# One 128x128 matrix in place of two parts of it, and a start in halves: a change to a two-layer decoder trunk

## The chip, the cores and the metric

The kernel is one program on one core of a Trainium2 chip. TensorE (PE in the rows) multiplies into PSUM, VectorE (DVE) and ScalarE (ACT) work on SBUF and PSUM, GpSimd (POOL) here only fills memory, and SyncE (SP) issues nearly all DMAs. Each engine runs its own instructions in order and waits for the others at semaphores. The metric is device time in microseconds.

## What is computed

Two layers over 256 tokens of width 1024, in float32. Each layer is a mixer with three branches (a short convolution, attention, and a delta rule with decaying state), a norm, a feed-forward part (dense in the first layer, two of eight experts in the second) and a norm. The change is about the delta rule and about the start of the first projection:

```python
def hybrid_mixer(x, w_in, ...):
    proj = x @ w_in
    (c_h, c_b, c_c, q, k, v, rr, rk, rv, wl, al, gl,
     g_conv, g_att, g_rwkv) = split_cols(proj, IN_SPLITS)
    ...

def delta_rule_scan(r, w, k, v, kk, a):
    def step(S, inp):
        r_t, w_t, k_t, v_t, kk_t, a_t = inp
        sa = jnp.einsum('bhvk,bhk->bhv', S, -kk_t)
        S = S * w_t[:, :, None, :] + sa[..., None] * (kk_t * a_t)[:, :, None, :] + v_t[..., None] * k_t[:, :, None, :]
        return S, jnp.einsum('bhvk,bhk->bhv', S, r_t)
    ...
    _, y = lax.scan(step, S0, xs)
```

## The kernel before

**Projections.** `x @ w_in` is worked off in units of 256 output columns. A unit's weight tile of 128 x 2048 (eight row blocks of 128 by 256 columns) is loaded by SyncE in two DMAs of 512 KB into one of three `raw` buffers. ScalarE copies it to `w_hi` (rounded), VectorE writes the rest, `raw - w_hi`, to `w_lo`, and TensorE makes each product as three (`mm3`, lines 471 to 473: hi by lo, lo by hi, hi by hi). A unit is two column blocks `m` of 128, each summed over eight row blocks `k` in one half of a PSUM bank `W[j % 3]`: 48 products. ScalarE then takes the bank out (`out_of_bank`, line 1163). The semaphores are `hi_done` and `lo_done` (tiles split so far), `w_used` (units multiplied so far) and `bank_free`. A tile is loaded two to three units ahead: the load of unit `u` waits until unit `u - 3` has been split (lines 323, 324). VectorE and ScalarE split unit `u + 2` while TensorE works on unit `u`.

**The order.** `TIMELINE` is a list written by hand. Each engine goes through it and does its own part of every entry. Small steps of the mixers stand between the units, or between a unit's first column block (`front`) and its second (`back`).

**The start.** SyncE issues, in this order: x part 0, first half of tile 0 (row blocks 0 to 3), x part 1, second half of tile 0, x parts 2 and 3, tile 1, the parameters, tile 2, a small weight, tile 3, the constants. ScalarE and VectorE split x in four parts and tile 0 in two halves. Tile 1 is split whole. TensorE's unit 0 runs the first column block over all `k`, waiting for the second half of the tile at `k = 4`, and then the second column block. After units 0, 1 and 2 comes `lora_w` (line 587), a product that needs `lora_in`: two ScalarE functions (lines 1203, 1204) on the result of unit 0, shifted by VectorE (`shift(6)`, lines 1676 to 1680). On VectorE that shift stands behind the split of tile 3.

**The delta rule.** It is done in two passes a layer, `p`, of four heads each, over two chunks `c` of 128 tokens. Every head and chunk (eight in a pass) has a triangular 128x128 matrix whose inverse is wanted. It is built in seven levels (`level`): two diagonal blocks of 64x64, and in the last level (`TOP`, lines 703 and 714) the block that joins them. They are kept transposed in `xt`, shape [128, 8, 2, 64], where the third index is the column half: `xt[0:64, :, 0]` and `xt[64:128, :, 1]` hold the diagonal blocks, `xt[0:64, :, 1]` the joining one. The lower diagonal block is made in `xt[64:128, :, 0]` and ScalarE copies it over (line 1318, `column_ready`). So `xt[64:128, :, 0]`, which would be zero in the transposed inverse, holds a used copy. VectorE writes the joining block (line 1792). Then, for each chunk, `cg` makes the right side and ScalarE copies it to `g_s`; `cu` applies the inverse to it; ScalarE copies that to `u_s`; `cy` makes output and state. `cu` therefore takes two products for each head: rows 0 to 63 of the result from partitions 0 to 63 of `xt` alone (line 738), rows 64 to 127 from all 128 partitions (line 739). There are eight `cu` groups in the kernel: two layers, two passes, two chunks.

In `TIMELINE`, `level(p, 6)`, `front` of a unit, `cg`, `back` of it and `cu` follow one another, and the same for the second chunk. GpSimd's program is five memsets at the start.

Of the kernel before, what the change touches and what calls it, by code (L numbers as in the profile page):

```python
# [32 lines left out]
P = 128  # L33
# [133 lines left out]
def trunk(nc, x, x_t, w_in, w_branch, w_out, w2, gate_w2, par, const, const_att, const_moe, ln_gb,  # L167
          router, ffn_gate, ffn_up, ffn_down, moe_gate, moe_up, moe_down, out):
    ctx = ExitStack()
    with ctx:  # L170
# [145 lines left out]
        def _(sp):  # L316
# [47 lines left out]
            def load_first_half(k, full):  # L364
                d = raw[0][:].rearrange("p (k c) -> p k c", k=KD)
                s = w_in[0][:, SEGMENTS[0][1]:SEGMENTS[0][1] + 256].rearrange("(k p) c -> p k c", p=P)
                sp.dma_start(d[:, k:k + 4, :], s[:, k:k + 4, :]).then_inc(sem(full), 16)

            load_x(0)
            load_first_half(0, "first_full0")  # L370
            load_x(1)
            load_first_half(4, "first_full1")
            load_x(2)
            load_x(3)
            for l in range(L):
                for kind, where, n, _ in SEGMENTS:
# [11 lines left out]
                    else:  # L388
                        for q in range(n):
                            if u + q:  # L390
                                load_cols(u + q, 0, w_in[l], where + 256 * (RKV[q] if kind == "rkv" else q))
# [76 lines left out]
        def _(pe):  # L468
# [22 lines left out]
            def proj_unit(u, j, fresh=None, parts=(0, 1)):  # L491

                if 0 in parts:
                    if u:
                        unit_ready(u)
                    else:
                        pe.wait_ge(sem("first_lo"), 1)
                    job_bank(j)
                bank = tiles(W[j % 3][:])
                wh, wl = (w[u % 3][:].rearrange("p (k c) -> p k c", k=KD) for w in (w_hi, w_lo))  # L500
                for m in parts:
                    c = slice(m * P, (m + 1) * P)
                    for k in range(KD):
                        if u == 0 and m == 0 and k == KD // 2:
                            unit_ready(0)
# [225 lines left out]
            def cu(l, p, c):  # L731
# [409 lines left out]
        def _(act):  # L1141
# [3 lines left out]
            def split_hi(u, i=0):  # L1145

                act.wait_ge(raw_full[u % 3], UD * (u // 3 + (1 if u % 3 else 0) + i))
# [10 lines left out]
            def out_of_bank(kind, q, u, j):  # L1158
# [3 lines left out]
                       "qkv": share[:, 2 * q:2 * q + 2, :]}.get(kind, sgate[:, (2 * q) % KD:(2 * q) % KD + 2, :])  # L1162
                A(dst, tiles(W[j % 3][:]), ACT.Sigmoid if kind.startswith("gate") else ACT.Copy)\
# [369 lines left out]
            act.wait_ge(sem("eps_ready"), 1)  # L1533
            def x_high(k):
# [3 lines left out]

            x_high(0)
            act.wait_ge(sem("first_full0"), 16)  # L1540
            A(w_hi[0][:, 0:UN // 2], raw[0][:, 0:UN // 2], ACT.Copy).then_inc(sem("first_hi"), 1)
            x_high(1)
            act.wait_ge(sem("first_full1"), 16)
            A(w_hi[0][:, UN // 2:UN], raw[0][:, UN // 2:UN], ACT.Copy).then_inc(hi_done, 1)
            x_high(2)
            x_high(3)
            split_hi(1)
# [54 lines left out]
        def _(pool):  # L1602
# [5 lines left out]
            nc.gpsimd.memset(s_s[:], 0.0).then_inc(sem("state_zero"), 1)  # L1608

# [3 lines left out]
        def _(dve):  # L1613
# [527 lines left out]
            def x_low(k):  # L2141
# [4 lines left out]

            x_low(0)
            dve.wait_ge(sem("first_hi"), 1)
            V.tensor_tensor(w_lo[0][:, 0:UN // 2], raw[0][:, 0:UN // 2], w_hi[0][:, 0:UN // 2].bitcast(F32), ALU.subtract)\  # L2149
                .then_inc(sem("first_lo"), 1)  # L2150
            x_low(1)
            dve.wait_ge(hi_done, 1)
            V.tensor_tensor(w_lo[0][:, UN // 2:UN], raw[0][:, UN // 2:UN], w_hi[0][:, UN // 2:UN].bitcast(F32), ALU.subtract)\
                .then_inc(lo_done, 1)
            x_low(2)
            x_low(3)
            split_lo(1)
# [102 lines left out]
```

## Time and profile before

| | us |
|---|---|
| median of 3 runs | 1743.91 |
| lowest and highest | 1743.23, 1744.04 |
| the profiled execution | 1743.99 |
| its span | 1741.9 |
| mean granted TensorE clock | 0.983 |

The span goes from the first to the last instruction; the profiled execution's own time is 2.1 us longer. TensorE is busy for 96% of the span, VectorE for 73%, ScalarE for 57%. In the timeline a product in fp32 that is not split stands as two passes of the same line, so `x8` of line 728 is four products. A busy time is that of the pipelined instruction from start to end; the pace of products is read from one start to the next. The three `mm3` lines of a unit start 0.12 us apart at the full clock.

### The profile page before, as it was taken

To read this page: it belongs to the slowest core of one execution; us is meant where nothing else is said; L and a number is where in the kernel's file an instruction comes from. 1 tells how busy PE (TensorE), PEld (TensorE's weight loads), DVE (VectorE), ACT (ScalarE), POOL (GpSimd) and SP (SyncE) were. 2 spreads that over 40 slices of the span, in tenths; PEclk is the share of its full clock that TensorE was granted. 3 is DMA by queue.
4 is the path that set the end of the run, shared out by engine and by line. 5 is a ranking of instruction groups with operands and counts; after the bars stand their busy time and mean duration, and the time that the engine had idled before them with its cause. 6 is when DMAs were issued, how large, how long until landed. Compare 5 with 4: busy or idle time off the path is not lost.

```text
span 1741.9 us, 30534 instructions
## 1 busy us (share of the span) xinstructions
PE 1680.4 (96%) x12126; PEld 1493.4 (86%) x12126; DVE 1274.5 (73%) x1217; ACT 1001.4 (57%) x967; POOL 0.9 (0%) x8
## 2 busy tenths in 40 slices
PE   7999999999999899999998999999999999999997
PEld 7899888889999889988987888888888888888886
DVE  5766666474444676656647889888998989888987
ACT  5553453453434555345344777777777777777775
POOL 0000000000000000000000000000000000000000
PEclk9999999999999899999998999999999999999999
DMA  9433332456656353333245999999998999899993
GB/s 285 146 98 119 100 121 75 163 170 193 187 174 213 126 163 105 98 121 122 75 145 207 340 333 392 333 371 368 346 386 325 374 331 392 333 367 350 368 385 142
DMA packets 253187, 411.19 MB, mean 236 GB/s; under 512 B 9376, under 2 KB 134688, under 8 KB 252576
## 3 DMA queue, kind: packets, MB, share of 16 engines
q1 hardware_dynamic: 250832, 400.97, 65.5%
q10 hardware_dynamic: 2256, 8.82, 1.4%
q8 instruction: 72, 1.18, 0.3%
q14 instruction: 27, 0.22, 0.0%
HBM read 407.66 MB, written 2.10 MB: 235 GB/s over the span
## 4 chain that ended last, share of the span: by engine, by line
PE 85%; DVE 7%; ACT 4%; issue 2%; DMA 1%; SPq 0%; ACTq 0%; DVEq 0%
PE W L471 18%; PE W L473 18%; PE W L472 18%; PE Y L471 6%; PE Y L472 6%; PE Y L473 6%; PE Y L675 3%; ACT w_hi L1150 2%; PE W L580 1%; DMA raw<-w_in 1%; DVE w_lo L1625 1%; DVE sc L1767 1%; PE Y L662 1%; PE Y L946 1%; PE Y L580 1%
## 5 line engine op out<-in xcount | busy, mean ns | idle before, releaser
L1625 DVE TENSOR_TENSOR w_lo<-raw,w_hi 128x2048 fp32r<-128x2048 f32 x114 | 261.2, 2292 | 218.2 <-ACT w_hi L1150 217.4
L471 PE MATMUL W<-w_lo,x_hi 128*128 128x512 f32 (+1 forms) x1120 | 390.3, 349 | 1.4 <-DVE x_lo L1928 1.1
L473 PE MATMUL W<-w_hi,x_hi 128*128 128x512 f32 (+1 forms) x1120 | 386.2, 345 | 0.0
L472 PE MATMUL W<-w_hi,x_lo 128*128 128x512 f32 (+1 forms) x1120 | 385.7, 344 | 0.0
L1632 DVE TENSOR_TENSOR w_lo<-raw,w_hi 128x2048 fp32r<-128x2048 f32 x144 | 329.6, 2289 | 44.9 <-ACT w_hi L1156 44.8
L1156 ACT ACTIVATE w_hi<-raw 128x2048 fp32r<-128x2048 f32 x144 | 276.0, 1917 | 73.3 <-PE Y L473 40.0
L471 PE MATMUL W<-x_lo,w_hi 128*128 128x256 f32 x992 | 296.8, 299 | 10.1 <-DVE w_lo L2149 8.9
L1632 DVE TENSOR_TENSOR w_lo<-raw_more,w_hi 128x2048 fp32r<-128x2048 f32 x120 | 274.9, 2291 | 28.7 <-ACT w_hi L1156 28.1
L472 PE MATMUL W<-x_hi,w_lo 128*128 128x256 f32 x992 | 286.4, 289 | 0.0
L473 PE MATMUL W<-x_hi,w_hi 128*128 128x256 f32 x992 | 285.9, 288 | 0.0
L1156 ACT ACTIVATE w_hi<-raw_more 128x2048 fp32r<-128x2048 f32 x120 | 230.5, 1921 | 64.0 <-PE W L473 41.3
L1150 ACT ACTIVATE w_hi<-raw 128x2048 fp32r<-128x2048 f32 x114 | 217.5, 1908 | 41.4 <-PE Y L473 31.2
L471 PEld LDWEIGHTS W<-w_lo,x_hi 128*128 128x128 f32 x1120 | 213.0, 190 | 26.8 <-issue 1.3
L473 PEld LDWEIGHTS W<-w_hi,x_hi 128*128 128x128 f32 x1120 | 212.8, 190 | 25.6
L472 PEld LDWEIGHTS W<-w_hi,x_lo 128*128 128x128 f32 x1120 | 213.0, 190 | 24.7
L471 PEld LDWEIGHTS W<-x_lo,w_hi 128*128 128x128 f32 x992 | 195.8, 197 | 19.1 <-DVE w_lo L2149 8.9
L472 PEld LDWEIGHTS W<-x_hi,w_lo 128*128 128x128 f32 x992 | 196.0, 198 | 1.3 <-issue 1.0
L473 PEld LDWEIGHTS W<-x_hi,w_hi 128*128 128x128 f32 x992 | 195.9, 198 | 0.0
L471 PE MATMUL Y<-w_lo,o_hi 128*128 128x512 f32 x440 | 172.3, 392 | 0.7 <-DVE o_lo L1942 0.7
L472 PE MATMUL Y<-w_hi,o_lo 128*128 128x512 f32 x440 | 171.5, 390 | 0.0
L473 PE MATMUL Y<-w_hi,o_hi 128*128 128x512 f32 x440 | 171.3, 389 | 0.0
L471 PEld LDWEIGHTS Y<-w_lo,o_hi 128*128 128x128 f32 x440 | 82.7, 188 | 17.4 <-DVE w_lo L1625 1.1
(318 smaller groups left out, 1929.7 us busy)
## 6 DMA issues: line engine op xcount, KB each, us to landing
raw<-w_in SPq DMA_DIRECT2D x124, 512.0 KB, 4.6
raw<-moe_gate SPq DMA_DIRECT2D x48, 1024.0 KB, 5.9
raw<-moe_up SPq DMA_DIRECT2D x48, 1024.0 KB, 6.3
raw<-moe_down SPq DMA_DIRECT2D x48, 1024.0 KB, 5.1
raw_more<-moe_gate SPq DMA_DIRECT2D x40, 1024.0 KB, 7.2
raw_more<-moe_up SPq DMA_DIRECT2D x40, 1024.0 KB, 6.7
raw_more<-moe_down SPq DMA_DIRECT2D x40, 1024.0 KB, 5.7
raw<-w_branch SPq DMA_DIRECT2D x24, 512.0 KB, 4.4
```

Source lines behind the costliest of these rows:

```text
L471: nc.tensor.matmul(out_ap, lhs[0], rhs[1], start=start, stop=False)
L472: nc.tensor.matmul(out_ap, lhs[1], rhs[0], start=False, stop=False)
L473: return nc.tensor.matmul(out_ap, lhs[0], rhs[0], start=False, stop=stop)
L580: return nc.tensor.transpose(out_ap, in_ap, ident)
L662: last = nc.tensor.matmul(Y[(1 + u + h) % 4][:, part], keys[rows, m, tc], ar[rows, m, c].rearrange("p s t -> p (s t)"), start=True, stop=True)
L675: last = nc.tensor.matmul(tiles(bank, 4)[half, u, :], left[half, 4 * c + u, :], right[half, 4 * c + u, :], start=True, stop=True)
L946: nc.tensor.matmul(out_ap, xs_lo[:, t, kk], picked, start=t == 0, stop=False)
L1150: A(w_hi[u % 3][:], raw[u % 3][:], ACT.Copy).then_inc(hi_done, 1)
L1156: A(w_hi[(u + x) % 3][:], landing(place_of(x))[:], ACT.Copy).then_inc(hi_done, 1)
L1625: V.tensor_tensor(w_lo[u % 3][:], raw[u % 3][:], w_hi[u % 3][:].bitcast(F32), ALU.subtract)\
L1632: V.tensor_tensor(w_lo[r][:], landing(place_of(x))[:], w_hi[r][:].bitcast(F32), ALU.subtract).then_inc(lo_done, 1)
L1767: mark(V.tensor_tensor(sc[:, u].rearrange("p (b s) t -> p b (s t)", b=2), tiles(Y[(1 + u) % 4][:]), si, ALU.mult), "score_ready", 8 * n + ...
```

## The change

1. `cu`: one product for each head with the whole of `xt[:, 4c+h]` as a 128x128 matrix, in place of two with parts of it. For this `xt[64:128, :, 0]` must be zero: GpSimd clears it with a memset in each of the four passes, after the column was copied and the last level's products have read it, and `cu` waits for that (`corner_clear`) and no longer for the copy.
2. Unit 0 on TensorE: both column blocks over row blocks 0 to 3, then both over 4 to 7. The second block's sum lies in `Y[0]`, so that ScalarE takes the unit out with two copies.
3. Tile 1 is split in halves like tile 0, each with a semaphore of its own, and unit 1 begins when the first half is split.
4. ScalarE makes a copy of one column of `small` ahead of everything.

```diff
-            def load_first_half(k, full):
-                d = raw[0][:].rearrange("p (k c) -> p k c", k=KD)
+            def load_first(u, k):
+                d = raw[u][:].rearrange("p (k c) -> p k c", k=KD)
+                col = SEGMENTS[u][1]
...
             load_x(0)
-            load_first_half(0, "first_full0")
+            load_first(0, 0)
             load_x(1)
-            load_first_half(4, "first_full1")
+            load_first(0, 4)
             load_x(2)
             load_x(3)
+            load_first(1, 0)
+            load_first(1, 4)
...
+                if u == 0:
+                    for half in range(2):
+                        if half:
+                            unit_ready(0)
+                        else:
+                            pe.wait_ge(sem("first_lo"), 1)
+                        for m, to in enumerate((bank[:, 0, :], tiles(Y[0][:])[:, 0, :])):
+                            c = slice(m * P, (m + 1) * P)
+                            for k in range(4 * half, 4 * half + 4):
+                                if m == 0:
+                                    x_part(0, k)
+                                last = mm3(to, (wh[:, k, c], wl[:, k, c]), (x_hi[:, k, :], x_lo[:, k, :]),
+                                           k == 0, k == KD - 1)
+                    last.then_inc(w_used, 1)
+                    return
+                if u == 1:
+                    pe.wait_ge(sem("first_lo"), 2)
+                elif 0 in parts:
+                    unit_ready(u)
...
                 if c == 0:
-                    pe.wait_ge(sem("column_ready"), n + 1)
+                    pe.wait_ge(sem("corner_clear"), n + 1)
                 for h, m, hc, half in HEADS:
-                    nc.tensor.matmul(Y[1][0:HD, hc], xt[0:HD, 4 * c + h, 0, :], g_s[0:HD, h, :], start=True, stop=True)
-                    last = nc.tensor.matmul(Y[1][HD:P, hc], xt[:, 4 * c + h, 1, :], g_s[:, h, :], start=True, stop=True)
+                    whole = xt[:, 4 * c + h].rearrange("p a b -> p (a b)")
+                    last = nc.tensor.matmul(Y[1][:, hc], whole, g_s[:, h, :], start=True, stop=True)
...
+                if u == 0:
+                    A(dst[:, 0, :], W[0][:, 0:T], ACT.Copy)
+                    A(dst[:, 1, :], Y[0][:, 0:T], ACT.Copy).then_inc(bank_free[0], 1)
+                    return
...
             act.wait_ge(sem("eps_ready"), 1)
+            A(small[:, 52:53], small[:, 9:10], ACT.Copy)
...
             x_high(3)
-            split_hi(1)
+            first_hi(1, 0)
+            first_hi(1, 4)
...
+            pool.wait_ge(sem("state_zero"), 1)
+            for n in range(2 * L):
+                if n:
+                    pool.wait_ge(sem("corner_clear"), n)
+                pool.wait_ge(sem("column_ready"), n + 1)
+                pool.wait_ge(sem("dxt_done"), 2 * TOP * (n + 1))
+                nc.gpsimd.memset(xt[HD:P, :, 0, :], 0.0).then_inc(sem("corner_clear"), 1)
```

TensorE at the first `cu` group, before: the last product of the unit's second block, then the products of the group (eight of them, two for each head; the first three stand here).

```order
L472 MATMUL W<-x_hi,w_lo_56 128x256
L473 MATMUL W<-x_hi,w_hi_53 128x256
L738 MATMUL Y<-gu_s,xt 64x64
L739 MATMUL Y<-gu_s,xt 64x64
L738 MATMUL Y<-gu_s,xt 64x64
```

The same place now, up to the next unit.

```order
L475 MATMUL W<-x_hi,w_lo_56 128x256
L476 MATMUL W<-x_hi,w_hi_53 128x256
L757 MATMUL Y<-gu_s,xt 128x64 x4
L474 MATMUL W<-x_lo,w_hi_54 128x256
L475 MATMUL W<-x_hi,w_lo_57 128x256
```

Nothing has moved here: eight products of at most 64 result rows have become four of 128.

ScalarE at the start, before; the names in brackets are the semaphores waited for.

```order
L1537 ACT_TABLE_LOAD [waits x_full0]
L1537 ACTIVATE x_hi<-xf 128x512 [waits eps_ready]
L1541 ACTIVATE w_hi_52<-raw_49 128x1024 [waits first_full0]
L1537 ACTIVATE x_hi<-xf 128x512 [waits x_full1]
L1544 ACTIVATE w_hi_52<-raw_49 128x1024 [waits first_full1]
L1537 ACTIVATE x_hi<-xf 128x512 [waits x_full2]
L1537 ACTIVATE x_hi<-xf 128x512 [waits x_full3]
L1150 ACTIVATE w_hi_53<-raw_50 128x2048 [waits raw_full1]
L1150 ACTIVATE w_hi_54<-raw_51 128x2048 [waits raw_full2]
```

ScalarE at the start now.

```order
L1556 ACT_TABLE_LOAD
L1556 ACTIVATE small<-small 128x1 [waits eps_ready]
L1560 ACTIVATE x_hi<-xf 128x512 [waits x_full0]
L1565 ACTIVATE w_hi_52<-raw_49 128x1024 [waits first_full00]
L1560 ACTIVATE x_hi<-xf 128x512 [waits x_full1]
L1565 ACTIVATE w_hi_52<-raw_49 128x1024 [waits first_full04]
L1560 ACTIVATE x_hi<-xf 128x512 [waits x_full2]
L1560 ACTIVATE x_hi<-xf 128x512 [waits x_full3]
L1565 ACTIVATE w_hi_53<-raw_50 128x1024 [waits first_full10]
L1565 ACTIVATE w_hi_53<-raw_50 128x1024 [waits first_full14]
L1168 ACTIVATE w_hi_54<-raw_51 128x2048 [waits raw_full2]
```

The table load no longer waits for x, and tile 1 is copied in two halves. VectorE's splits follow in the same order.

## Rows read from the trace of the kernel before

**Rows 1.** The page: busy time by engine, and the chain's shares by engine

```profile
PE 1680.4 (96%) x12126; PEld 1493.4 (86%) x12126; DVE 1274.5 (73%) x1217; ACT 1001.4 (57%) x967; POOL 0.9 (0%) x8
...
PE 85%; DVE 7%; ACT 4%; issue 2%; DMA 1%; SPq 0%; ACTq 0%; DVEq 0%
```

**Rows 2.** The chain of waits at the groups: start us, us, what

```profile
185.43 0.45 PE Y L580 x4
...
193.38 0.70 DVE rkvl L1755
...
865.48 0.26 PE Y L738 x2
```

**Rows 3.** The chain of waits at the start

```profile
11.28 9.21 DMA raw<-w_in
...
20.51 1.92 ACT w_hi L1150
```

**Rows 4.** Timeline, start: start us, us, engine, line, operation [idle before <-releaser]

```profile
4.73 1.28 ACT L1537 ACT_TABLE_LOAD   x1 [4.73 <-DMA xf<-x_t]
...
6.56 1.04 ACT L1541 ACTIVATE w_hi<-raw 128x1024 fp32r<-128x1024 f32 x1
...
8.91 0.58 PE L471 MATMUL W<-x_lo,w_hi 128*128 128x256 f32 x1 [8.91 <-DVE w_lo L2149]
...
17.20 0.39 PE L471 MATMUL W<-x_lo,w_hi 128*128 128x256 f32 x1 [0.55 <-DVE w_lo L1625]
...
29.70 1.10 PE L587 MATMUL E<-rkvl,w_s 128*128 128x256 f32 x4 [0.73 <-ACT rkvl L1204]
```

**Rows 5.** Line 739's weight loads: ns min/median/max, first and last start

```profile
L739 PEld LDWEIGHTS Y<-gu_s,xt x64: 132/134/136, 154.2 to 881.5; 128*64 128x64 f32 x64
```

**Rows 6.** Timeline of TensorE at the first cu group

```profile
153.74 0.28 PE L473 MATMUL W<-x_hi,w_hi 128*128 128x256 f32 x1
153.95 0.33 PE L738 MATMUL Y<-gu_s,xt 64*64 64x64 f32 x2
...
156.00 0.39 PE L471 MATMUL W<-x_lo,w_hi 128*128 128x256 f32 x1
```

**Rows 7.** Timeline of TensorE at the first cg group

```profile
150.10 1.00 PE L728 MATMUL Y<-vtok,sc 128*128 128x64 f32 x8
150.90 0.37 PE L471 MATMUL W<-x_lo,w_hi 128*128 128x256 f32 x1
```

**Rows 8.** Waits in the expert stage, 945 to 1742: us, times, longest

```profile
ACT w_hi L1156 <- PE W L473: 74.6, 84, 3.0
```

**Rows 9.** Timeline: GpSimd's memset, and the corner's last reads and first use

```profile
1.19 0.31 POOL L1608 MEMSET s_s<- 128x256 f32 x1
...
144.56 1.14 PE L714 MATMUL Y<-xt,mc 64*64 64x64 f32 x16 [1.20 <-ACT mc L1315]
...
289.12 0.67 PE L714 MATMUL Y<-xt,mc 64*64 64x64 f32 x8 [0.18 <-ACT mc L1315]
...
296.54 0.33 PE L738 MATMUL Y<-gu_s,xt 64*64 64x64 f32 x2
```

**Rows 10.** The two DMAs of tile 0: issue ns, first and last issue; landing

```profile
L367 SPq DMA_DIRECT2D raw<-w_in x2: 419/426/434, 1.2 to 2.2; - x2
...
DMA to landing us min/median/max: 4.8/5.5/6.2
```

**Rows 11.** Stretches: us, busy (count) of PE, PEld, DVE, ACT, POOL, PEclk, DMA share, GB/s

```profile
8.90:12.70 3.80, 3.79 (x17) 3.79 (x18) 2.99 (x4) 1.67 (x3) 0.00 (x0) 1.00 1.09 351
...
194.30:198.00 3.70, 3.68 (x30) 3.37 (x31) 3.56 (x6) 3.00 (x4) 0.00 (x0) 1.00 0.37 131
...
241.20:244.80 3.60, 3.53 (x18) 3.53 (x19) 2.03 (x1) 1.27 (x4) 0.00 (x0) 0.54 0.60 213
```

**Rows 12.** Timeline of TensorE: a short wait and a longer one

```profile
194.32 0.70 PE L662 MATMUL Y<-ar,t_b 64*128 64x256 f32 x4 [0.64 <-DVE rkvl L1755]
...
241.27 0.74 PE L580 MATMUL Y<-cst,pr 128*128 128x128 f32 x3 [2.32 <-ACT pr L1339]
```

More of the change, by code:

```diff
@@ L389, in _ @@
                         for q in range(n):
-                            if u + q:
+                            if u + q > 1:
                                 load_cols(u + q, 0, w_in[l], where + 256 * (RKV[q] if kind == "rkv" else q))
@@ L491, in proj_unit @@
             def proj_unit(u, j, fresh=None, parts=(0, 1)):
[L493 to L498, printed above, removed]
                 bank = tiles(W[j % 3][:])
                 wh, wl = (w[u % 3][:].rearrange("p (k c) -> p k c", k=KD) for w in (w_hi, w_lo))
+                if u == 0:
[17 more added lines that the diff above has]
+                    unit_ready(u)
+                if 0 in parts:
+                    job_bank(j)
                 for m in parts:
@@ L503, in proj_unit @@
                     for k in range(KD):
-                        if u == 0 and m == 0 and k == KD // 2:
-                            unit_ready(0)
+                        if u == 1 and m == 0 and k == KD // 2:
+                            unit_ready(1)
                         if fresh is not None and m == 0:
@@ L1145, in split_hi @@
             def split_hi(u, i=0):
-                act.wait_ge(raw_full[u % 3], UD * (u // 3 + (1 if u % 3 else 0) + i))
+                act.wait_ge(raw_full[u % 3], UD * (u // 3 + (1 if u % 3 == 2 else 0) + i))
                 if u >= 3:
@@ L1537, in x_high, with first_hi @@
                 A(x_hi[:, c, :], xf[:, c, :], ACT.Copy).then_inc(sem("x_hi_ready"), 1)
+            def first_hi(u, k):
+                c = slice(256 * k, 256 * k + UN // 2)
+                act.wait_ge(sem(f"first_full{u}{k}"), 16)
+                A(w_hi[u][:, c], raw[u][:, c], ACT.Copy).then_inc(hi_done if k else sem("first_hi"), 1)
             x_high(0)
-            act.wait_ge(sem("first_full0"), 16)
-            A(w_hi[0][:, 0:UN // 2], raw[0][:, 0:UN // 2], ACT.Copy).then_inc(sem("first_hi"), 1)
+            first_hi(0, 0)
             x_high(1)
-            act.wait_ge(sem("first_full1"), 16)
-            A(w_hi[0][:, UN // 2:UN], raw[0][:, UN // 2:UN], ACT.Copy).then_inc(hi_done, 1)
+            first_hi(0, 4)
             x_high(2)
             x_high(3)
-            split_hi(1)
+            first_hi(1, 0)
+            first_hi(1, 4)
             handlers = {"units": units, "front": front, "back": back, "lora_in": lora_in, "rate_w": rate_w, "rate_a": rate_a,
@@ L2145, in x_low, with first_lo @@
                     .then_inc(sem("x_lo_ready"), 1)
+            def first_lo(u, k):
+                c = slice(256 * k, 256 * k + UN // 2)
+                if k:
+                    dve.wait_ge(hi_done, u + 1)
+                else:
+                    dve.wait_ge(sem("first_hi"), u + 1)
+                low = V.tensor_tensor(w_lo[u][:, c], raw[u][:, c], w_hi[u][:, c].bitcast(F32), ALU.subtract)
+                low.then_inc(lo_done if k else sem("first_lo"), 1)
             x_low(0)
-            dve.wait_ge(sem("first_hi"), 1)
-            V.tensor_tensor(w_lo[0][:, 0:UN // 2], raw[0][:, 0:UN // 2], w_hi[0][:, 0:UN // 2].bitcast(F32), ALU.subtract)\
-                .then_inc(sem("first_lo"), 1)
+            first_lo(0, 0)
             x_low(1)
-            dve.wait_ge(hi_done, 1)
-            V.tensor_tensor(w_lo[0][:, UN // 2:UN], raw[0][:, UN // 2:UN], w_hi[0][:, UN // 2:UN].bitcast(F32), ALU.subtract)\
-                .then_inc(lo_done, 1)
+            first_lo(0, 4)
             x_low(2)
             x_low(3)
-            split_lo(1)
+            first_lo(1, 0)
+            first_lo(1, 4)
             dve.wait_ge(sem("prm_full"), 16)
```

4 lines of the change are left out of this document (2 added, 2 removed).

## The prediction

> **What bounds the kernel now.** I read the page of the profile first, then the waits, the chain of waits, and the timeline. The page gives TensorE 96% of the span and 85% of the chain [rows 1], so a microsecond taken from TensorE's program is a microsecond of the kernel wherever the chain runs through TensorE, and nothing where TensorE then waits for a time that somebody else sets. That is the question to ask at both places of the change. At the eight groups of products that apply the inverted triangle, the chain runs through the very instructions that are replaced [rows 2]. At the start it does not: it runs through a DMA that lands at 20.49 us, a ScalarE copy, a VectorE shift, and ends in a TensorE wait at 29.70 [rows 3, 4].
>
> **Part 1: eight groups of products.** Before, each group is four heads of two products, and each fp32 product stands as two passes in the trace: line 739 alone has 64 passes, 8 groups times 4 heads times 2, and line 738 has as many [rows 5]. The first group begins at 153.95 and the next product at 156.00 [rows 6]: 2.05 us for 16 passes, 0.128 us each. The other seven groups read the same to 0.01 us. After, a group is four products of a 128x128 weight with 64 columns, 8 passes. The kernel has that form already, line 728, same shapes and types: 150.10 to 150.90 for 8 passes, 0.80 us, 0.100 each [rows 7]. So a group saves 2.05 - 0.80 = 1.25 us, and eight save 10.0 us. The bounds: if the new passes keep the old pace of 0.128, a group costs 1.02 and eight save 8.2 us. And the old group also has a longer step at its head than line 728 (0.21 us from the product before it to 153.95, where 0.12 is usual); if that step was due to the change of shape and goes, another 0.09 us a group, 10.7 us in all. I take 10.0, since line 728 is the same form and only the step at the edges is open.
>
> The trace shows TensorE's weight load at 134 ns for 64 columns [rows 5] and line 728 still starting a pass each 100 ns. The Trainium skill (TensorE: Matmul & The Clock Gate, LDWEIGHTS) says that a load takes its columns over 1.2 GHz, whatever the rows: by that the loads of a group cost 16 x 53 ns before and 8 x 107 ns after, the same 0.85 us, and a kernel bound by loads would gain nothing. The rows of before stand at 2.05 us a group, so the old group is not at that floor, and a new one at 0.80 to 0.85 would be.
>
> Does the saving arrive? After each group TensorE goes on with the next unit's projections, whose weights VectorE has split two units ahead, and the next small step, which needs ScalarE's copy of the group's result, stands half a unit (some 2.9 us) later, while the copy takes 0.4 us. The later TensorE waits (for VectorE's bonus, ScalarE's probabilities, the normalised rows) are all started by TensorE work behind the groups: in the chain each leaves TensorE and comes back to it, as from the transposes at 185.43 over VectorE's bonus at 193.38 to the scores at 194.32 [rows 2, 12]. They move with it and stay as long. The DMA of the expert stage is busy, but ScalarE's waits there name TensorE, not a DMA [rows 8], so that stage moves as a whole.
>
> **Part 2: the corner.** GpSimd is idle after the start, so its four new memsets delay nobody on its own queue. TensorE's wait moves from the ScalarE copy of the column to the memset behind it. Nearest price: a memset of 128x256 took 0.31 us [rows 9]; the corner is 64 partitions of 512 elements, twice the length, so some 0.6 us, between 0.3 and, if the strided form is ten times dearer, 6. It can start when the last level's products have read the corner and the column is copied, 145.7 in the first pass and 289.8 in the second [rows 9]; TensorE needs it at 153.95 and 296.54. The cover is 8.2 and 6.7 us, made of two half units of projections and one small step. Cost 0. If the cover were gone, TensorE would stop in front of the group with everything behind it. VectorE runs a PSUM copy and fp32 products beside the memset; slowed by its full 0.6 us, it would still be ahead of TensorE, which needs nothing of it for two units.
>
> **Part 3: the start.** ScalarE loads its table at 4.73, when x has landed, and so copies x only at 6.03 [rows 4]. The new tiny copy draws that load to before the landing. The first weight half lands at 1.21 + 4.8 = 6.01 [rows 10], so its copy can start at 6.05 and not at 6.56, and TensorE's first product moves from 8.91 to about 8.4: 0.5 us, not the 1.28 of the load. Until 12.7 TensorE runs 17 products in 3.79 us, 0.22 each, later 0.12 [rows 11]; the half us at the slow pace is worth about 0.25. Using the first half for both output blocks before the second half is wanted removes a 0.1 us wait on x; the second tile split in halves removes the 0.55 us wait at 17.20 [rows 4], since its halves would be ready near 13.8 and 15.2. Together TensorE reaches the product on line 587 about 0.9 to 1.1 us earlier, at 28.0 in place of 28.97.
>
> That product waits until 29.70, and the chain behind that wait is not touched: the fourth tile's load is issued at 10.87, when the second half of the first tile is split (that half lands at 2.22 + 6.2 = 8.42 as before), lands at 20.49, ScalarE copies it for 1.92, VectorE splits it and only then makes the shift that ScalarE's two functions need [rows 3, 4, 10]. SyncE's queue has the same DMAs in the same order. So the wait grows from 0.73 to about 1.8 us and the start gives 0. The extra 0.25 us of ScalarE for taking out unit 0 in two copies lies in its wait for that DMA.
>
> The longer wait has a price of its own. After a wait of 2.32 us that ended at 241.27 the granted clock of the next 3.6 us was 0.54, nearly all of it at 1.2 GHz; after one of 0.64 at 194.32 it stayed at 1.00, 2.4 GHz [rows 11, 12]. A wait of 1.8 lies between. If the clock falls as it did there, TensorE loses 0.46 x 3.6 = 1.7 us, and TensorE is the chain behind line 587, so the loss stays.
>
> **The sum** against the profiled execution: 1743.99 - 10.0 = 1734.0. The median of the runs is 0.08 below that execution, so 1733.9.
>
> **The rivals.**
> A, forecast: the groups give 10.0, the start 0, the clock holds. 1733.9. Chance 0.50.
> B, the same with the clock falling after the wait at 29.70: + 1.7, 1735.6. For it, the nearest longer wait; against it, the nearest shorter one. 0.32.
> C, the saving arrives only in part: a VectorE or ScalarE stretch between two groups turns out to be the limit and takes back half. The chain has 11% on these two engines. 1743.9 - 5.0 = 1738.9. 0.09.
> D, no gain in the groups: a whole product costs what its two parts cost together, 0.256 us a pass, since they shared the array. 1743.9. The trace speaks against it: passes of the two shapes start 0.128 apart, and the whole form at line 728 takes 0.100. 0.06. The Trainium skill (TensorEngine Tiling (Array Packing), Theoretical Speedup and Key Properties) has this rule: products of contraction 64 or less can be tiled for up to twice the speed, tiles working in parallel, which filling up with zeros gives away. The same list says that a change of tiling mode drains TensorE, and the old group changes it at every product; that fits the slow 0.128.
> E, slower: the memset is late. The first group of each of the four passes waits for it. The cover is 8.2 or 6.7 us; to lose the 10.0 and 3.5 more, four waits of 3.4 us are needed, so a memset of 10 to 11.6 us, over 30 times the 0.31 us row. It would then give 1747.4 or more. 0.03.
>
> **How the numbers follow.** A and B hold 0.82 and span, with the bounds of the pace (8.2 to 10.7) and the spread of the runs of before (0.8 us), from 1732.3 to 1737.9. The range is 1732.0 to 1738.0. A measurement of this kernel can tell about 0.2%, 3.5 us, from no change: faster is below 1740.4, which A, B and C are, 0.91; D is the same, 0.06; E is slower, 0.03.
>
> **What would show it.** Right: a group with 8 passes in about 0.8 us; memsets of xt near 146 and 290, ending far ahead of the group; the table load near 1 us; the first product near 8.4; no wait at the second tile; line 587 still near 29.70 with a wait of about 1.8 us in front. The granted clock just behind it decides between A and B. The gap to before at the start of layer two's first group should be 5.0 us (or 3.3) and grow by 1.25 with each. Wrong: passes at 0.2 us or more (D); waits elsewhere that grew by what the groups saved (C); a TensorE wait for GpSimd (E); or line 587 starting earlier, which would mean that the DMA chain did move.

## The result, and the profile after

| | before, us | changed, us |
|---|---|---|
| median of 5 runs each | 1743.54 | 1733.06 |
| lowest and highest | 1741.51, 1744.04 | 1732.62, 1738.47 |
| ratio (95% interval) | | 0.995 (0.9934 to 0.9965) |
| the profiled execution | 1743.99 | 1738.47 |
| its span | 1741.9 | 1736.5 |

The changed kernel is 10.5 us faster by the medians, 6.1 to 11.5 by the interval. The forecast was 1733.9, in a range from 1732.0 to 1738.0. One thing needs care: the profiled execution of the changed kernel is the slowest of its five, 5.4 us above the median. What it shows of the groups is the same in a second profile of the same kernel; what it shows of the start is not, as that profile says below.

The page of the changed kernel (busy time by engine, the chain's shares by engine), against [rows 1]: TensorE's busy time is 7.1 us less and GpSimd's 2.1 more, and the chain has the same shares.

```profile
PE 1673.3 (96%) x12062; PEld 1491.1 (86%) x12062; DVE 1275.3 (73%) x1218; ACT 1002.1 (58%) x970; POOL 3.0 (0%) x12
...
PE 85%; DVE 7%; ACT 4%; issue 2%; DMA 1%; SPq 0%; DVEq 0%; ACTq 0%
```

The timeline of TensorE at the first `cu` group, against [rows 6].

```profile
158.00 0.28 PE L476 MATMUL W<-x_hi,w_hi 128*128 128x256 f32 x1
158.12 1.00 PE L757 MATMUL Y<-gu_s,xt 128*128 128x64 f32 x8
158.93 0.36 PE L474 MATMUL W<-x_lo,w_hi 128*128 128x256 f32 x1
159.13 0.28 PE L475 MATMUL W<-x_hi,w_lo 128*128 128x256 f32 x1
```

Eight passes take 0.81 us (158.12 to 158.93), and the longer step at the head is gone: 0.12 us from the product before, where it was 0.21. From the unit's last product to the second product of the next unit it is 1.13 us; in [rows 6] it is 153.74 to 156.22, the second product standing 0.22 us behind the row at 156.00, so 2.48. The difference of 1.35 us, eight times, is 10.8 us; all eight groups read alike, in both kernels.

GpSimd's clearing and the start in the same profile: the first row is the memset of the first pass, the others stand against [rows 4].

```profile
150.14 0.53 POOL L1642 MEMSET xt<- 64x512 f32 x1 [148.62 <-PE Y L732]
```

```profile
0.75 1.28 ACT L1556 ACT_TABLE_LOAD   x1 [0.75 <-PEq L2293]
...
8.63 0.58 PE L474 MATMUL W<-x_lo,w_hi 128*128 128x256 f32 x1 [8.63 <-DVE w_lo L2187]
...
31.32 2.05 PE L605 MATMUL E<-rkvl,w_s 128*128 128x256 f32 x4 [3.10 <-ACT rkvl L1226]
```

The memset takes 0.53 us and is done 7.5 us ahead of the group at 158.12. The table load stands at the beginning, and TensorE has no wait between unit 0 and unit 1. But the product that needs `lora_in` (line 605, which was 587) starts at 31.32, 1.62 us later than before, behind a wait of 3.10. In the windows of this profile (columns as in [rows 11]) the granted clock is at its lower level right behind that wait.

```profile
31.30:34.80 3.50, 3.48 (x12) 3.14 (x13) 1.73 (x1) 3.50 (x5) 0.00 (x0) 0.50 0.49 171
34.80:38.20 3.40, 3.40 (x22) 3.40 (x21) 3.29 (x6) 1.24 (x1) 0.00 (x0) 0.64 0.36 95
```

0.50 is 1.2 GHz for the whole stretch. The two together, the late start and the clock, put this execution 4.3 us behind the one of before at the next wait that both have. The first row is of before, the second of the changed kernel, where line 685 has become 703.

```profile
82.64 0.68 PE L685 MATMUL Y<-cst,xt 64*64 64x64 f32 x16 [2.37 <-DVE xt L1775]
86.96 0.68 PE L703 MATMUL Y<-cst,xt 64*64 64x64 f32 x16 [2.37 <-DVE xt L1809]
```

### The profile page after: what moved, and what is told of

It is laid out like the page before. It is cut to its first block, busy times and chain, and to the rows that moved or that the text cites. A ratio compares the mean times of both kernels' runs of the same rounds, so it can differ in the third digit from the quotient of the medians.

```text
span 1736.5 us, 30417 instructions
## 1 busy us (share of the span) xinstructions
PE 1673.3 (96%) x12062; PEld 1491.1 (86%) x12062; DVE 1275.3 (73%) x1218; ACT 1002.1 (58%) x970; POOL 3.0 (0%) x12
## 4 chain that ended last, share of the span: by engine, by line
PE 85%; DVE 7%; ACT 4%; issue 2%; DMA 1%; SPq 0%; DVEq 0%; ACTq 0%
PE W L474 18%; PE W L476 18%; PE W L475 18%; PE Y L474 6%; PE Y L475 6%; PE Y L476 6%; PE Y L693 3%; ACT w_hi L1168 2%; PE W L598 1%; DMA raw<-w_in 1%; DVE w_lo L1659 1%; DVE sc L1801 1%; PE Y L598 1%; PE Y L680 1%; PE Y L964 1%
```

## Experiments: which part gives the time

**The groups alone.** The start of before, the change of `cu` and the clearing.

```diff
-                    nc.tensor.matmul(Y[1][0:HD, hc], xt[0:HD, 4 * c + h, 0, :], g_s[0:HD, h, :], start=True, stop=True)
-                    last = nc.tensor.matmul(Y[1][HD:P, hc], xt[:, 4 * c + h, 1, :], g_s[:, h, :], start=True, stop=True)
+                    whole = xt[:, 4 * c + h].rearrange("p a b -> p (a b)")
+                    last = nc.tensor.matmul(Y[1][:, hc], whole, g_s[:, h, :], start=True, stop=True)
```

> Part 1 and 2 of the change alone: the eight cu groups as four whole products each and the corner cleared by GpSimd, on the start of the kernel before. Theory G (the gain is the eight groups and nothing else): a group takes 0.81 us in place of 2.05 plus 0.09 less at its head, so 8 x 1.35 = 10.7 us, 1732.8 for a before of 1743.5, and the wait at the product after unit 2 stays near 0.7 us with the clock holding behind it. Rival S (the start gives something too, some 0.5 us or more): then this is slower than the whole change. Rival W (the start costs, since its longer wait lowers the clock): then this is as fast or up to 3 us faster than the whole change.

Measured: 1733.34 us, median of 6, against 1742.34 of before (17 runs, which four of the kernels are compared with), ratio 0.995 (0.9936 to 0.9963). The whole gain is here: the whole change has 1733.09 beside the same runs of before (below). In this profile the wait at line 587 was 1.13 us and not near 0.7, and ended at 30.21; the clock held behind it (1.00).

**The start alone.** The changed kernel with the old `cu` and no clearing.

> The rest of the change alone: the early table load, unit 0 in halves over both column blocks, tile 1 split in halves; cu and the corner as before. Theory G: the time of before to within 0.5 us, the first product near 8.5, the product behind unit 2 (29.70 before) unmoved, with the wait in front of it grown from 0.7 to about 1.8 us. Rival W: the same wait, but the granted clock falls behind it in a good part of the executions, 1.7 to 3.4 us more, median 1744 to 1746. Rival S: up to 1 us faster than before.

Measured: 1740.73 us, median of 12, ratio 0.9995 (0.9985 to 1.0005). The medians differ by 1.6 us, but the interval goes from 2.6 us faster to 0.9 slower, so the start on its own can't be told from nothing. In its timeline the first product is at 8.50, and line 605 stands where it stood before, with a longer wait:

```profile
29.96 1.10 PE L605 MATMUL E<-rkvl,w_s 128*128 128x256 f32 x4 [1.69 <-ACT rkvl L1226]
```

**The changed kernel once more**, for a second profile of its start.

> The changed kernel once more beside its two parts, for a second profile and more times. The first profile had line 605 start at 31.32 where before had 29.70, the fourth tile landing 1.6 us later, a wait of 3.1 us in front and 6.8 us at the half clock behind. If that was one execution's DMA (theory G), this profile has the tile landing near 20.5 again and a wait near 1.8. If the change makes the loads land later (rival L), it shows near 22 again, and in the profile of the start alone too. Time: 10 to 11 us below before, 1733.

Measured: 1733.09 us, median of 6 (1730.76 to 1736.12), ratio 0.9949 (0.9934 to 0.9964). The timeline at the same places, and a window behind the wait:

```profile
29.81 1.10 PE L605 MATMUL E<-rkvl,w_s 128*128 128x256 f32 x4 [2.69 <-ACT rkvl L1226]
```

```profile
82.75 2.04 PE L703 MATMUL Y<-cst,xt 64*64 64x64 f32 x32 [2.38 <-DVE xt L1809]
```

```profile
29.80:33.20 3.40, 3.39 (x25) 3.30 (x26) 1.63 (x1) 3.40 (x5) 0.00 (x0) 1.00 0.96 320
```

Here the fourth tile's chain is on time, line 605 starts at 29.81 and the clock stays at 2.4 GHz though the wait was 2.69 us. At line 703 the execution stands at 82.75 where before stood at 82.64: in these two executions the start has given nothing and cost nothing. So the 4.3 us of the first profile belong to that execution. Its chain of waits, against [rows 3], shows the first part of it, the load of tile 3 issued and landed later:

```profile
12.43 9.66 DMA raw<-w_in
...
22.12 1.93 ACT w_hi L1168
```

The load ran from 12.43 to 22.09, in [rows 3] from 11.28 to 20.49: it began 1.15 us later and took 0.45 us longer. In the second profile and in that of the start alone the tile landed at 20.6 and 20.7, so the new start is not what delays it. The rest, 4.3 - 1.6 = 2.7 us, fits the clock: by the two windows above it takes 0.50 x 3.5 + 0.36 x 3.4 = 3.0 us.

## Experiments: the wait at the start

**Both small steps earlier.** `shift(6)` and `lora_in` both before unit 1 in the order, so that the wait goes.

```diff
-    ("units", "lora", 0, 1), ("units", "rkv", 0, 1),
-    ("shift", 6), ("lora_in",),
+    ("units", "lora", 0, 1), ("shift", 6), ("lora_in",),
+    ("units", "rkv", 0, 1),
```

> The changed kernel with the shift of unit 0's result and its two ScalarE functions put one entry earlier in the order, ahead of the split of tile 3 on VectorE and ScalarE. If the wait in front of line 605 is the chain of the fourth tile's load, copy and split ahead of the shift, then the product comes right behind unit 2, near 27.8, without a wait, and the clock holds: 2 us (the next unit then starts at about 28.9, when tile 3 is split, and not at 31.2) to 3.7 us below the changed kernel, about 1730. Rival: the work is only moved, VectorE and ScalarE are late at the next tiles, and the time is that of the changed kernel.

Measured: 1730.7 us, median of 6 (1728.99 to 1735.8), ratio 0.9935 (0.992 to 0.995). TensorE and ScalarE in the timeline:

```profile
25.01 1.28 ACT L1226 ACT_TABLE_LOAD   x1
...
26.63 1.89 ACT L1168 ACTIVATE w_hi<-raw 128x2048 fp32r<-128x2048 f32 x1
...
26.87 1.10 PE L605 MATMUL E<-rkvl,w_s 128*128 128x256 f32 x4
...
30.97 0.39 PE L474 MATMUL W<-x_lo,w_hi 128*128 128x256 f32 x1 [3.00 <-DVE w_lo L1659]
```

The wait at line 605 is gone and has come back one step later: ScalarE makes two DMA issues, a table load and two functions before it copies tile 3, so the copy begins at 26.63 and TensorE waits 3.00 us for the unit itself. The median is 2.4 us below that of the changed kernel beside it (1733.09), but the two sets of runs overlap, and the profiled execution, 1735.8, is the slowest of the six.

**VectorE's step earlier, ScalarE's left where it was.**

```diff
-    ("units", "lora", 0, 1), ("units", "rkv", 0, 1),
-    ("shift", 6), ("lora_in",),
+    ("units", "lora", 0, 1), ("shift", 6), ("units", "rkv", 0, 1),
+    ("lora_in",),
```

> The changed kernel with only VectorE's shift of unit 0 moved ahead of its split of tile 3; ScalarE's two functions stay where they were, behind its copy of tile 3. Moving both had only changed which wait TensorE meets: ScalarE spent 4 us (two DMA issues, a table load, two functions) ahead of the copy of tile 3, and unit 3 waited 3.0 us for its split. Here the copy of tile 3 comes first (20.6 to 22.5), the functions end near 25.7, the split near 24.8, so TensorE meets neither: the product on line 605 comes at about 27.2 and unit 3 near 28.5, not 31.3. Then 2 to 2.7 us below the changed kernel, about 1730.5, and more where its clock had fallen there. Rival: something later in the first 60 us (a tile's load, ScalarE's functions for the rates) takes the 2 us back; then 1733.

Measured: 1730.86 us, median of 6 (1727.81 to 1734.54), against 1741.77 of before (11 runs, which four of the kernels are compared with), ratio 0.9942 (0.9924 to 0.9959). Now TensorE has no wait up to a short new one at 48.07, and line 703 stands 1.75 us earlier than in the changed kernel's second profile (82.75):

```profile
48.07 1.09 PE L636 MATMUL E<-cst,inv 128*64 128x128 f32 x16 [0.83 <-DVE inv L1756]
81.00 0.68 PE L703 MATMUL Y<-cst,xt 64*64 64x64 f32 x16 [2.39 <-DVE xt L1809]
```

**The same shift with the start of before**, to see whether the new start gives anything once the wait is gone.

> The groups and the corner of the change and the earlier shift on VectorE, but the start of the kernel before. If the start's 1 us was hidden by the wait behind unit 2, it shows now: this is 1 us (up to 1.5) slower than the same with the new start, about 1731.7. If the start gives nothing at all, the two are the same.

Measured: 1730.69 us, median of 6 (1727.64 to 1732.02), ratio 0.9935 (0.9918 to 0.9952). Against the groups alone (1731.99 to 1733.91), which it is but for the shift, the runs hardly overlap: this is the clearest sign that the shift saves time, 2.7 us by the medians and 2.1 if each is taken against its own runs of before. By the runs the new start gives nothing even so. The timeline of this kernel has the waits that the new start removes, and the later row to compare with 81.00 (line 685 here is 703 there):

```profile
11.86 0.55 PE L471 MATMUL W<-x_lo,w_hi 128*128 128x256 f32 x1 [0.44 <-DVE x_lo L2151]
...
17.47 0.39 PE L471 MATMUL W<-x_lo,w_hi 128*128 128x256 f32 x1 [0.69 <-DVE w_lo L1632]
```

```profile
81.93 0.68 PE L685 MATMUL Y<-cst,xt 64*64 64x64 f32 x16 [2.38 <-DVE xt L1782]
```

So the start's gain is there once nothing waits behind it, 0.93 us at this place in these two executions. That is less than six runs of each can show, and whether it reaches the end stays open.

## Experiments: what the products cost, and the cover of the corner

**Two products of all 128 rows.** Each whole product is split by columns of the matrix, both halves with all 128 partitions. The result is the same, since the corner is zero.

```diff
-                    whole = xt[:, 4 * c + h].rearrange("p a b -> p (a b)")
-                    last = nc.tensor.matmul(Y[1][:, hc], whole, g_s[:, h, :], start=True, stop=True)
+                    nc.tensor.matmul(Y[1][0:HD, hc], xt[:, 4 * c + h, 0, :], g_s[:, h, :], start=True, stop=True)
+                    last = nc.tensor.matmul(Y[1][HD:P, hc], xt[:, 4 * c + h, 1, :], g_s[:, h, :], start=True, stop=True)
```

> The changed kernel with each head's whole product taken apart again into two column halves, but both over all 128 partitions (the corner is zero), so all 16 passes of a group have the one shape 128x64 by 64. Theory D (the old group was slow, 0.128 us a pass, because it changed between a 64-row and a 128-row shape at every product): the pace is 0.10 us, a group 1.6 us, and the kernel 8 x 0.8 = 6.4 us above the changed one, 1739.5. Rival N (a pass with 64 weight columns takes 0.128 whatever its rows): 2.05 us a group, 8 x 1.24 = 9.9 us above, 1743. Rival H (half the columns, half the time: 0.05 us): no slower than the changed kernel.

Measured: 1731.71 us, median of 6 (1727.86 to 1735.84), ratio 0.9938 (0.9921 to 0.9954). Of what I had expected only rival H, no slower than the changed kernel, is left; D and N, 6.4 and 9.9 us slower, are out. The timeline of TensorE at the first group:

```profile
154.06 0.28 PE L476 MATMUL W<-x_hi,w_hi 128*128 128x256 f32 x1
154.27 0.27 PE L756 MATMUL Y<-gu_s,xt 128*64 128x64 f32 x1
154.28 0.27 PE L757 MATMUL Y<-gu_s,xt 128*64 128x64 f32 x1
154.38 0.22 PE L756 MATMUL Y<-gu_s,xt 128*64 128x64 f32 x1
154.38 0.22 PE L757 MATMUL Y<-gu_s,xt 128*64 128x64 f32 x1
154.44 0.22 PE L756 MATMUL Y<-gu_s,xt 128*64 128x64 f32 x1
154.44 0.22 PE L757 MATMUL Y<-gu_s,xt 128*64 128x64 f32 x1
...
154.74 0.22 PE L757 MATMUL Y<-gu_s,xt 128*64 128x64 f32 x1
154.89 0.39 PE L474 MATMUL W<-x_lo,w_hi 128*128 128x256 f32 x1
155.11 0.28 PE L475 MATMUL W<-x_hi,w_lo 128*128 128x256 f32 x1
```

The passes of the two lines start in pairs, within 0.01 us of each other, a pair each 0.06 us: the two halves of the columns work at the same time. Rival H had them one behind the other at 0.05 us, which would be 0.8 us a group. Sixteen passes take 0.62 us, and the step from edge to edge (154.06 to 155.11) is 1.05 us against 1.13 for the whole products and 2.48 for the old ones, though the old ones have as many passes and fewer rows. So neither the number of passes, nor their 64 columns, nor the turn from one column half to the other made the old group slow. What is left is that it mixes products of 64 and of 128 rows.

**The shapes apart.** The kernel before, with one line more: the four products of 64 rows first, then the four of 128.

```diff
                 for h, m, hc, half in HEADS:
                     nc.tensor.matmul(Y[1][0:HD, hc], xt[0:HD, 4 * c + h, 0, :], g_s[0:HD, h, :], start=True, stop=True)
+                for h, m, hc, half in HEADS:
                     last = nc.tensor.matmul(Y[1][HD:P, hc], xt[:, 4 * c + h, 1, :], g_s[:, h, :], start=True, stop=True)
```

> The kernel before with one thing changed: in each cu group the four products of 64 rows come first and the four of 128 rows behind them, in place of the two shapes by turns. The same 16 passes. Theory that the pace of 0.128 us comes from the change of row shape between neighbours: only one change is left in a group, so the passes of one shape run at the pace of their own kind. They lie on the same columns, so they cannot run side by side as the equal shapes did; 16 passes at 0.06 to 0.10 give 1.0 to 1.6 us a group in place of 2.05, so 0.4 to 1.0 us less a group and 3 to 8 us less in all, 1735 to 1739. Rival, that a product of 64 columns out of these parts costs 0.128 whatever stands beside it: the group stays 2.05 us and the time at 1742.5.

Measured: 1734.87 us, median of 5 (1731.55 to 1736.88), against 1742.34 of before (12 new runs, the next kernel's too), ratio 0.9959 (0.9942 to 0.9976). The timeline of TensorE:

```profile
151.81 0.28 PE L473 MATMUL W<-x_hi,w_hi 128*128 128x256 f32 x1
152.01 0.68 PE L738 MATMUL Y<-gu_s,xt 64*64 64x64 f32 x8
152.62 0.68 PE L740 MATMUL Y<-gu_s,xt 128*64 128x64 f32 x8
153.23 0.39 PE L471 MATMUL W<-x_lo,w_hi 128*128 128x256 f32 x1
153.45 0.28 PE L472 MATMUL W<-x_hi,w_lo 128*128 128x256 f32 x1
```

The same sixteen passes, with one change of shape inside the group, take 1.22 us and not 2.05: eight of either kind in 0.61 us. From edge to edge it is 1.64 us, 0.84 less than before, 6.7 us over eight groups; the medians differ by 7.5. The old order changes the shape seven times inside a group and this one once, so a change costs about (2.05 - 1.22) / 6 = 0.14 us (an estimate). So a program that clears nothing and multiplies nothing more gets about six tenths of the gain by the timeline (6.7 of 10.8 us), by the order of eight instructions; the medians can't give the share more closely. The whole matrix takes the rest: half the passes, 0.81 us in place of 1.22, and no longer step at the head.

**Both of the best together.** Two products of all rows, and VectorE's shift before unit 1.

> The changed kernel with both improvements that the earlier runs pointed to: each head's product in cu as two products of 128 rows and 64 columns side by side, and VectorE's shift(6) placed before unit 1. If the two are independent, their savings add: the two products take 0.62 us a group where the whole one takes 0.81 with the step at its head kept at 0.21 instead of 0.12, so about 0.1 us a group, 0.8 in all, below the version with the shift alone (1730.9), so about 1730. The theory that the earlier median of the two products alone (1731.7 against 1733.1) was mostly spread gives the same number. The rival that the two products really save 1.4 us and more would give 1729.4 or less. In the trace: no TensorE wait for lora_in at line 605, groups of 0.62 us.

Measured: 1729.19 us, median of 6 (1726.99 to 1735.12), ratio 0.9931 (0.9912 to 0.9949). The fastest median of all, 13 us below before and some 4 below the change. If its parts add, 1730 was expected; the number fits, but the runs overlap with those of the version with the shift alone (1727.81 to 1734.54), so it doesn't show it.

**The clearing made dearer.** Twenty memsets of the corner in each pass in place of one, each behind the one before; `cu` waits for the last of them. The result stays the same.

```diff
-                nc.gpsimd.memset(xt[HD:P, :, 0, :], 0.0).then_inc(sem("corner_clear"), 1)
+                for r in range(20):
+                    if r:
+                        pool.wait_ge(sem("corner_clear"), 20 * n + r)
+                    nc.gpsimd.memset(xt[HD:P, :, 0, :], 0.0).then_inc(sem("corner_clear"), 1)
```

> The changed kernel with the corner's memset done 20 times in a row, each behind the one before, in each of the four passes: some 20 x 0.6 = 12 us of GpSimd in place of 0.53. Theory: a single clear is free because TensorE needs it some 8 us (first pass) and 6 us (second pass) after it can start; with 12 us TensorE waits for it, about 4 us in the first pass and 6 in the second, in both layers, 20 us in all and some 2 to 5 more for the clock, about 1755. Rival: if GpSimd's stores slowed VectorE beside them, VectorE's fp32 instructions between would be longer than before (0.69 us for 128x512, 2.29 for 128x2048), and the loss larger.

Measured: 1756.57 us, median of 4, ratio 1.0085 (1.0065 to 1.0104). The waits of TensorE (engine, line, waited for: us in total, times, longest), and the first of them in the timeline:

```profile
PE Y L757 <- POOL xt L1645: 16.8, 4, 5.0
```

```profile
148.50 11.58 POOL L1645 MEMSET xt<- 64x512 f32 x20 [146.98 <-PE Y L732]
```

```profile
160.22 1.81 PE L757 MATMUL Y<-gu_s,xt 128*128 128x64 f32 x8 [2.74 <-POOL xt L1645]
```

One memset costs 0.58 us with its wait. Of four times 11.6 us, 16.8 arrive as waits, so the mean cover is 7.4 us; against the changed kernel's 1733.09 the whole cost is 23.5 us, 6.7 more than the waits. The clock can account for that: the mean of these four runs is 0.979, of the changed kernel's six 0.983, and 0.4% of the time is some 7 us (an estimate). The group behind the wait shows one such place: its eight passes are busy for 1.81 us where they were for 1.00, and the window from there on has a granted clock of 0.54:

```profile
160.20:162.20 2.00, 1.98 (x10) 2.00 (x11) 0.00 (x0) 0.14 (x1) 0.00 (x0) 0.54 1.05 365
```

The rival, that GpSimd's stores slow VectorE beside them, holds for one form of instruction and costs little. VectorE's instructions on two tiles are as long beside the memsets as without (0.69 us for 128x512, 2.29 for 128x2048). The `TENSOR_SCALAR` of 128x256 is not: 0.35 us each without, 0.44 to 0.69 beside them. The first row is of this kernel, the second of the changed kernel's second profile:

```profile
151.56 1.11 DVE L1779 TENSOR_SCALAR t_g<-t_g,prm 128x256 f32<-128x256 f32 x2
149.47 0.62 DVE L1776 TENSOR_SCALAR t_g<-t_g,prm 128x256 f32<-128x256 f32 x2
```

## Why the prediction was right

**Part 1, the groups.** The mechanism and the place were right. The pace of line 728 was the right row: 0.81 us for eight passes against 0.80. The term was a little small, since I left the step at the head out of the middle value: with it the group saves 1.35 us and the sum is 10.8, at the upper bound I had named (10.7). The forecast by it would have been 1733.1, and the medians of the two sets of runs are 1733.06 and 1733.09. That this is so close is partly luck: the median of before was 1743.54 in one set and 1742.34 in the other, so the change measured 10.5 and 9.25 us, and the medians can't choose between 10.0 and 10.8. The trace does. That the saving arrives is shown by the groups alone, 9.0 us by the medians. Rival C, a wait elsewhere that takes it back, is out: TensorE's longest waits in all are as before, 7.3 us in the four at line 580 (7.2 in the groups alone) and 5.2 in the four at line 685 (5.2). The gap to before at layer two's first group, forecast at 5.0 us, is 4.9 in the second profile (718.11 against 723.04) and 2.8 in the first, and grows by 1.35 with each group.

**What the old pace was.** I had taken 0.128 us a pass as a given. The two runs on it show what it was made of: changes of row shape from one product to the next. Rival D asked whether the two parts shared the array in time. They did not, as parts of different shape; parts of the same shape do. The Trainium skill (TensorEngine Tiling (Array Packing), Key Properties) says that a switch of tiling mode drains TensorE, and that different tiles can load weights and multiply in parallel. The trace agrees that a switch costs time, 2.05 against 1.22 us, though a drain is not seen as such, and that tiles in different columns run together, with starts 0.01 us apart. The fastest kernel here fills up with zeros and tiles all the same, so filling up does not by itself give the parallel tiles away. The rule on loads that I cited from the Trainium skill (TensorE: Matmul & The Clock Gate, LDWEIGHTS) would have given 0.85 us, an estimate, for the sixteen loads and for the eight. The eight took 0.81, the sixteen 0.62 when their columns lay side by side, so it does not bound passes on different columns.

**Part 2, the corner.** Right: 0.53 us against the 0.6 estimated, and free. The cover of 8.2 and 6.7 us is borne out by the twenty memsets: longest wait 5.0 us behind a chain of 11.5, so 6.5 us where it is shortest. Rival E needed a memset of 10 us or more and is 19 times away from it.

**Part 3, the start.** Right that it gives nothing as the kernel stands, and for the reason given: in the second profile line 605 stands at 29.81 and in the start alone at 29.96, against 29.70, whatever TensorE gained ahead of it. The wait grew from 0.73 us to 2.69 in the one and 1.69 in the other, where I had 1.8. The first product was to be at 8.4: 8.63, 8.19 and 8.50 in three profiles. But this does not bear out the 0.5 us that I gave the early table load: the three profiled kernels with the old start that I ran later (the groups alone, the shift with it, the shapes apart) have 8.40, 8.49 and 8.51, and x landed at 4.22 to 4.33 there, at 4.73 in the profile of before. So part of the 8.91 was a late landing of x, and the early load is worth 0.2 to 0.3 us. What the start saves ahead of the wait lies in the waits for x and for tile 1 (0.44 and 0.69 us in the old start above). What I had not seen either is that the DMA chain behind the wait varies by as much as the whole part is worth: the load of tile 3 is issued when the second half of tile 0 has been split, so a late landing of that half moves the chain, and did, by 1.15 of the 1.6 us, in the first profile. My number for this chain came from a single execution.

**The clock, A against B.** It differs from execution to execution, and the length of the wait does not settle it. Behind the wait of 3.10 us the clock fell, behind 2.69 it did not, behind the 3.00 us of the run with both steps earlier it fell (0.61 in the window 31.0 to 34.4). But it also fell behind waits that were shorter than 2.69: the 2.32 us of [rows 11, 12], and 2.10 us at line 605 in the run with twenty memsets, whose start is that of the changed kernel:

```profile
30.32 1.73 PE L605 MATMUL E<-rkvl,w_s 128*128 128x256 f32 x4 [2.10 <-ACT rkvl L1226]
```

```profile
30.30:33.70 3.40, 3.38 (x13) 3.11 (x14) 1.62 (x1) 3.40 (x5) 0.00 (x0) 0.55 0.84 280
```

So A and B are not two outcomes for the kernel but two kinds of its executions, and placing a wait of 1.8 us between 0.64 and 2.32, as I did, says nothing of which of the two it will be. The medians lie nearer A, but with runs spread over 5 us they can't tell the 1.7 us between the two. What decides it in one execution stays open.

**The range.** It held the median, but its reason was poor. By the terms that I named its ends come to 1732.4 and 1738.2, not 1732.3 and 1737.9. And I took 0.8 us as the spread of a kernel's runs, from the three that I had. Beside the experiments, in three sets of runs, the kernel before ran from 1736.93 to 1746.32 us, 7.6 to 8.0 us apart within a set. A good part of that is the clock at places that the change does not touch. The stretch from 143 to 153 us has the same program in both kernels up to the memset; the first row is of before, the second of the changed kernel's second profile:

```profile
143.00:153.00 10.00, 8.80 (x72) 8.60 (x70) 9.11 (x14) 4.68 (x7) 0.00 (x0) 0.83 0.34 107
```

```profile
143.00:153.00 10.00, 8.80 (x57) 8.55 (x56) 9.04 (x14) 4.49 (x7) 0.53 (x1) 0.66 0.33 105
```

TensorE is as busy, but its granted clock is 0.66 in place of 0.83, which by 0.17 x 10 is 1.7 us less of work. From the end of the stretch's first wait (144.56, now 144.37) to the `cg` group behind it (line 728, now 746; 150.10, now 151.41) it is 7.04 us in place of 5.54, 1.5 longer.

Each run on record has its span and its mean granted clock. Their product is an estimate of the span at the full clock, and it takes most of the scatter away: over 40 runs of before its standard deviation is 1.3 us, that of the times 2.2. The clock is on record in steps of 0.001, or 1.7 us a run, so only means of several runs are of use. The last column is an interval of 95%.

| | runs | mean of span x clock, us | below before, us |
|---|---|---|---|
| before | 40 | 1713.2 | |
| the start alone | 12 | 1713.0 | 0.3 (-0.3 to 0.9) |
| the shapes apart | 5 | 1707.3 | 5.9 (5.0 to 6.8) |
| the groups alone | 6 | 1702.4 | 10.8 (10.0 to 11.7) |
| the changed kernel once more | 6 | 1702.4 | 10.8 (10.2 to 11.5) |
| two products of all rows | 6 | 1700.6 | 12.6 (11.8 to 13.4) |
| VectorE's shift, old start | 6 | 1700.8 | 12.4 (11.4 to 13.5) |
| VectorE's shift, new start | 6 | 1700.2 | 13.0 (12.3 to 13.6) |
| both of the best | 6 | 1698.2 | 15.0 (14.4 to 15.5) |

By this estimate the groups give the 10.8 us of the timeline, the start nothing, the order of the shapes over half of the gain, the shift 1.6 and 2.2 us more, and the two best steps add.

## What to carry to other kernels

Products that use parts of the array are to be ordered by shape: where 64-row and 128-row products take turns, each pays for the change, and putting the equal ones together is free. Where filling up with zeros makes the shapes equal, compare the whole product with two column halves of it side by side; the halves were the shorter in the trace here, by 0.08 us a group, which the times of the runs can't tell apart. And before a start-up is tuned, look for the next time that somebody else sets: the gain of a stage that ends in a wait for a DMA chain is nothing until that chain moves, and here moving one small VectorE step ahead of a tile's split took that wait away.

## What the runs showed of the hardware

- Sixteen fp32 passes of 64 columns: 2.05 us with 64 and 128 rows by turns, 1.22 with the shapes apart, 0.62 with 128 rows throughout and the two column halves by turns. Eight passes of 128 columns: 0.81 us.
- The length of TensorE's wait does not decide the granted clock behind it: at the same line 2.69 us left it at 1.00, while 2.10 us was followed by 3.4 us at 0.55 and 3.10 us by 3.5 us at 0.50.
- GpSimd's memset of 64 partitions by 512 floats in strides takes 0.53 us; 128 by 256 took 0.31 [rows 9]. Beside it VectorE's `TENSOR_SCALAR` of 128x256 took 0.44 to 0.69 us in place of 0.35; its instructions on two tiles were not slowed.
- The executions of one and the same program, the kernel before, lie up to 9.4 us apart (1736.93 to 1746.32, three sets of runs). Span times granted clock scatters by 1.3 us where the times scatter by 2.2, so the clock is the larger part of it. In the changed kernel the landing of one early load differed by 1.6 us between two executions. What else there is stays open.
